# Two heads' matmuls into one PSUM bank: by token block, or head by head

## What is computed

```python
cb = jnp.einsum('bclgn,bcsgn->bcgls', c_c, b_c)
y_diag = jnp.einsum('bcgjls,bcsgjp->bclgjp', cb[:, :, :, None] * decay, xdt)
...
y = y + xs.astype(f32) * jnp.repeat(d_skip.astype(f32), SSD_HEAD_DIM)
g = (y * jax.nn.silu(z.astype(f32))).reshape(bsz, L, SSD_GROUPS, SSD_D_INNER // SSD_GROUPS)
g = g * lax.rsqrt(jnp.mean(g * g, axis=-1, keepdims=True) + EPS)
```

## Time and profile before

| | |
|---|---|
| median of 3 runs | 1215.65 us (1210.93 to 1218.96) |
| the profiled execution | 1215.65 us |
| its span, first to last instruction | 1214.0 us |
| mean granted clock of TensorE | 0.978 |
| TensorE busy over the span | 1153.8 us, 95% |
| VectorE busy over the span | 792.1 us, 65% |
| the change's function runs | from 64.7 to 233.4 us, eight times |

### The profile page before, as it was taken

One profiled execution on the slowest core, in us unless ns is written; L12 is line 12 of the kernel. 1 busy time (PEld: TensorE's weight loads), 2 busy tenths in 40 slices (PEclk: granted clock), 3 DMA queues, 4 the chain that ended last, 5 costly groups with the idle time before them and its releaser, 6 DMA issues.

```text
span 1214.0 us, 23710 instructions
## 1 busy us (share of the span) xinstructions
PE 1153.8 (95%) x8898; PEld 1091.7 (90%) x8898; DVE 792.1 (65%) x1219; ACT 646.9 (53%) x975; POOL 182.9 (15%) x134
## 2 busy tenths in 40 slices
PE   6999998999999999679898999999999999999998
PEld 5988898899999999556668999999998999999998
DVE  4999999868665453546546666555677578666543
ACT  5676677555554344457725555444544565555332
POOL 0343443317000001022302000000000211000000
PEclk9999999999999999889979999999999999999999
DMA  5644444384554544222204555555544455555553
GB/s 202 196 143 156 142 137 160 109 255 158 183 174 163 188 160 152 96 95 88 70 18 139 190 177 186 191 181 183 173 140 136 143 177 188 181 184 189 190 178 99
DMA packets 53224, 190.31 MB, mean 157 GB/s; under 512 B 5920, under 2 KB 7072, under 8 KB 53168
## 3 DMA queue, kind: packets, MB, share of 16 engines
q1 hardware_dynamic: 51408, 182.95, 45.4%
q0 software_dynamic: 1760, 6.59, 1.8%
HBM read 188.44 MB, written 1.08 MB: 156 GB/s over the span
## 4 chain that ended last, share of the span: by engine, by line
PE 77%; DVE 13%; ACT 5%; issue 3%; DVEq 1%; DMA 0%; ACTq 0%; POOL 0%; SPq 0%
PE lin L412 23%; PE lin L414 23%; PE lin L413 23%; DVE dd L1289 2%; DVE cv L1264 2%; DVE w_lo L1185 2%; PE lin L641 1%; PE ps L682 1%; PE ps L683 1%; ACT w_hi L824 1%; PE lin L639 1%; DVE mm L1314 1%; PE ps L756 1%; PE ps L779 1%; DVE x_tok L1306 1%
## 5 line engine op out<-in xcount | busy, mean ns | idle before, releaser
L1185 DVE TENSOR_TENSOR w_lo<-w_raw,w_hi 128x1024 fp32r<-128x1024 f32 x303 | 372.2, 1230 | 261.2 <-ACT w_hi L824 260.5
L824 ACT ACTIVATE w_hi<-w_raw 128x1024 fp32r<-128x1024 f32 (+2 forms) x343 | 355.0, 1040 | 265.3 <-PE lin L414 263.1
L412 PE MATMUL lin<-x_hi,w_hi 128*128 128x256 f32 (+1 forms) x1528 | 445.9, 292 | 10.9 <-DVE x_lo L1211 3.7
L414 PE MATMUL lin<-x_hi,w_lo 128*128 128x256 f32 (+1 forms) x1528 | 439.4, 288 | 0.0
L413 PE MATMUL lin<-x_lo,w_hi 128*128 128x256 f32 (+1 forms) x1528 | 438.8, 287 | 0.0
L412 PEld LDWEIGHTS lin<-x_hi,w_hi 128*128 128x128 f32 x1528 | 292.4, 191 | 15.5 <-DVE x_lo L1211 4.1
L413 PEld LDWEIGHTS lin<-x_lo,w_hi 128*128 128x128 f32 x1528 | 292.0, 191 | 1.5 <-issue 1.0
L414 PEld LDWEIGHTS lin<-x_hi,w_lo 128*128 128x128 f32 x1528 | 292.8, 192 | 0.0
L414 PE MATMUL lin<-hid_hi,w_lo 128*128 128x256 f32 (+1 forms) x768 | 218.2, 284 | 0.0
L413 PE MATMUL lin<-hid_lo,w_hi 128*128 128x256 f32 (+1 forms) x768 | 218.0, 284 | 0.0
L412 PE MATMUL lin<-hid_hi,w_hi 128*128 128x256 f32 (+1 forms) x768 | 217.5, 283 | 0.0
(11 more groups left out here) (252 smaller groups left out, 1522.1 us busy)
## 6 DMA issues: line engine op xcount, KB each, us to landing
w_raw<-w SPq DMA_DIRECT2D x343, 512.0 KB, 3.3
acs_bc<-acs_dram POOLq DMA_DIRECT2D x8, 544.0 KB, 4.9
bias_mask<-rpb POOLq DMA_DIRECT2D x4, 512.0 KB, 9.5
h<-h SPq DMA_DIRECT2D x4, 272.0 KB, 4.4
out<-h SPq DMA_DIRECT2D x8, 128.0 KB, 3.2
cst<-const SPq DMA_DIRECT2D x1, 784.0 KB, 8.8
vecs<-vec SPq DMA_DIRECT2D x1, 131.5 KB, 2.2
acs_dram<-y POOLq DMA_DIRECT2D x1, 34.0 KB, 2.3
```

What stands on the lines that cost most here:

```text
L412: mm3(o, wh, xh, start=first and i == 0, stop=False)
L414: ins = mm3(o, wl, xh, start=False, stop=last and i == kts - 1)
L824: a(w_hi[pg.slot][:, 0:n], w_raw[pg.slot][:, 0:n], ACT.Copy).then_inc(w_hi_done, pages)
L1185: tt(w_lo[pg.slot][:, 0:n], w_raw[pg.slot][:, 0:n], w_hi[pg.slot][:, 0:n].bitcast(F32), ALU.subtract)\
```

## The change

In each bank, the before kernel issues the first token block of both heads, then the second of both, then the third of both. The changed kernel issues the three blocks of one head, then the three of the other. The wait for `mm_done` is inside the head loop, with the same value for both heads. `y_done` is raised by the last matmul of the second head, as before.

```diff
-                    pe.wait_ge(mm_done, g.times(2, q + 1).value)
-                    halves = [(slice(e * HD, (e + 1) * HD), 2 * q + e) for e in range(2)]
-                    for rows, j in halves:
-                        nc.tensor.matmul(o[rows, 0:T], x_tok[:, 0, j * HD:(j + 1) * HD], mm[:, j, 0:T],
-                                         start=True, stop=False)
-                    for rows, j in halves:
-                        nc.tensor.matmul(o[rows, 128:T], x_tok[:, 1, j * HD:(j + 1) * HD], mm[:, j, T:416],
-                                         start=False, stop=False)
-                    for rows, j in halves:
-                        ins = nc.tensor.matmul(o[rows, 256:T], x_tok[0:META, 2, j * HD:(j + 1) * HD],
-                                               mm[0:META, j, 416:432], start=False, stop=True)
+                    for e in range(2):
+                        j = 2 * q + e
+                        pe.wait_ge(mm_done, g.times(2, q + 1).value)
+                        rows = slice(e * HD, (e + 1) * HD)
+                        cs = slice(j * HD, (j + 1) * HD)
+                        nc.tensor.matmul(o[rows, 0:T], x_tok[:, 0, cs], mm[:, j, 0:T], start=True, stop=False)
+                        nc.tensor.matmul(o[rows, 128:T], x_tok[:, 1, cs], mm[:, j, T:416], start=False, stop=False)
+                        ins = nc.tensor.matmul(o[rows, 256:T], x_tok[0:META, 2, cs], mm[0:META, j, 416:432],
+                                               start=False, stop=True)
                     ins.then_inc(y_done, 1)
```

## The result

| | before | changed |
|---|---|---|
| median of 15 runs each | 1216.53 us (1210.93 to 1218.96) | 1222.0 us (1216.36 to 1227.52) |
| ratio, 95% interval | | 1.0054 [1.0038, 1.0070] |
| the profiled execution, and its span | 1215.65 and 1214.0 us | 1221.69 and 1220.0 us |
| mean granted clock | 0.978 | 0.979 |
| one group's products, first to last | 2.15 us | 4.24 us |

Half a per cent slower, clear of the noise and within 1%, and within 0.6 us of the forecast of 1221.4. The two medians are 5.5 us apart, where 5.7 were forecast. The page of the changed kernel, beside the earlier trace rows: TensorE is busy 13.4 us longer over a span that is 6.0 longer.

What follows compares the result with a forecast made beforehand. VectorE was taken to pace the scan at 24.98 us a slot, until the lengthened loop through TensorE takes 25.88. Delays of 6.8 less 1.1 us of waits give 1215.65 + 5.7 = 1221.4 us; range 1215 to 1230.5.

Steps and rivals of the forecast that it cites:

- The pair costs what one costs: In `y_products`, two heads' matmuls run side by side; a lone head takes 1.075 us, a group 4.30 instead of 2.15.
- The 16-row matmul keeps the heads apart: In `y_products`, TensorE drains between 128 and 16 rows, so head 1 waits for head 0: +2.15 us per group.
- rival (a): In `y_products`, the heads still overlap despite the new order: no change, 1215.7 us; chance 0.13.
- The loop, 25.88 us: Scan slot: the chain TensorE, ScalarE, VectorE and back grows from 23.73 to 25.88 us, 0.90 longer than VectorE's pace.
- TensorE's own need, 25.07 us: Scan slot: TensorE's busy 22.92 us plus 2.15 makes 25.07, so it still waits 0.8 us at L492.
- rival (b): Scan: the loop is looser, nearly all added time is hidden and TensorE's 25.07 us counts: 1217.9 us; chance 0.12.
- Idle before L492 0.8 us, and no fall of the clock: Scan slots 2 to 7: TensorE idles about 0.8 us before L492 and the clock doesn't fall to 0.50.
- Slot by slot: Scan: delay grows to 0.6, 4.0, 4.7, then 6.8 us; vanished weight-load waits take off 1.1, leaving 5.7.
- The end: Behind the last group's L492 (244.44 us before) TensorE leads and everything shifts along: 5.7 us, 1221.4 us in all.
- (c): Scan: the clock falls to 1.2 GHz in every slot, 1.53 us each, 9.2 more: 1230.6 us; chance 0.10.
- (d): Scan: all added TensorE time is paid, 17.2 us over eight groups: 1232.9 us; chance 0.05.
- The second loop: Scan slot: the loop through VectorE's wait for bank 1's y (L1333) takes 25.5 us and decides nothing.

Runs made afterwards that it cites:

- The repeats: Kernel before with the first block of both heads issued once more, or twice more, per bank: ratios 1.0033 and 1.0026.
- three kernels of the table: Before, first block issued two times more; changed, 16-row matmuls last and first block issued twice; changed itself: slots 25.57, 25.67, 25.84 us.
- The changed kernel with GpSimd moved: Changed kernel with ScalarE's third page conversion behind the tap, one `w_lo` behind the clamp, another in the next slot: ratio to before 0.9958.
- the first repeat: Kernel before with the first block of both heads issued once more per bank: 3.06 us per group, ratio 1.0033.
- the second experiment: Changed kernel with the 16-row matmul made one of 128 rows, zeros added: ratio to before 1.0009.

## Why the prediction was right, step by step

- **The pair costs what one costs.** Right. One head alone takes 1.06 us (1.075 predicted) where two heads took 1.08. The group went to 4.24 us (4.30). The repeats show it from the other side: two more fp32 matmuls of 128x272 in a bank cost one's time, 0.91 us per group of two banks.
- **The 16-row matmul keeps the heads apart.** Right, and shown by taking it away from between them (2.16 us). Left out was a second reason: with 128 rows everywhere the new order still takes 2.47 us against 1.75, since head 1 starts only with head 0's third pass. That would have made rival (a) dearer than "no change" in the products, though not in the time.
- **The loop, 25.88 us.** Right to 0.04. By L492 of slots 3 to 7, 212.46 - 109.08 = 103.38 us in four slots (103.52 predicted, 100.16 before). That it is this loop is shown by cutting it with the clamp kept clear (25.84 to 25.21), and its constant by three kernels of the table (21.59 to 21.60 against 21.58). That VectorE sets the pace of the kernel before was right for its slots of 24.98 us alone; the two behind a fall of the clock were the loop's already, which is why they grow by 0.6 us and the others by 0.86.
- **TensorE's own need, 25.07 us.** A little high. The changed kernel with GpSimd moved shows 24.76 at products of 4.24, 0.3 less than forecast. The 22.92 of the earlier trace rows, which I added to, is of a slot that begins behind a wait, and in the kernel without waits this isn't paid; that this is the reason is likely and not shown. It decided nothing, but rival (b) rested on it, and by 24.76 it would have been cheaper still: no cost at all in the slots.
- **Idle before L492 0.8 us, and no fall of the clock.** Right: 0.78 to 0.82 in slots 3 to 7 (0.96 in slot 2), and 1.00 over 84 to 210 us.
- **Slot by slot.** Behind L492 of slot 2, the next slot took 0.58 us more (0.66 predicted), the four steady ones 3.22 together (3.36), slot 7 to 8 0.59 (0.7), and slot 8 to the last L492 0.89 (1.05, the products less the two waits; no wait on `g_lo` or `w_lo` is left there). Sum 5.28 us against 5.7. Each term was a little large, in part because the head's 1.075 was. The last L492 came at 249.03, not near 250.1, by these 0.4 us and by a lead of 0.69 (next point).
- **The end.** The 5.28 us aren't all of the 6.0 by which the spans differ. The changed kernel reached L492 of slot 2 0.69 us sooner, with a lead that it had before the first products, and took 1.44 us longer behind the last L492 (970.99 to 969.55), where its profile has 44.4 us at 1.2 GHz after 480 us and that of before 37.5. Both lie outside what was changed, and the second varies from run to run. So the 6.0 us between the two profiles are partly chance. The 5.5 between the medians of 15 runs are nearer to the 5.28 and bear the forecast better; that they meet the 5.7 to 0.2 us is within the noise of the medians.
- **Rivals.** (a) fell by the length of the products, (b) by the slots, (c) by the clock of 1.00. (d), all of it paid, fell by the first repeat, 0.91 us per group for nothing in the slots. (b) wasn't far off: two moves, of one conversion and of one `w_lo`, bring the slot from 25.84 to 25.21.
- **The second loop.** The one through VectorE's wait for `y` of bank 1 I had put at 25.5 us and as deciding nothing. It decided nothing, but the sum was wrong: the 13.9 from L1278 to L492 held the wait of 0.52 at the convolution. It measures 24.85. There is a wait of 0.67 us for this `y` in each of four slots, and the wait at the convolution behind it is there all the same. This loop became the one that paces as soon as the conversion was moved, which the forecast for that experiment didn't see.

## What to carry to other kernels

Two matmuls on the two column halves ran for the price of one here only where they stood close to each other in TensorE's program with no change of row count between them; issue them side by side, block by block. Ask what a slot's other loops hold before you price added time: 0.91 us per group cost nothing in the slots here, 2.09 (4.24 less 2.15) cost 0.86 per slot, and both follow from one sum along the chain from TensorE through the converting engine and back. When you sum such a loop, leave out the waits inside it. An engine's busy time is no lower bound of its pace when a neighbour's work holds its instructions up, as GpSimd's did VectorE's; and moving that work may mostly choose which instruction pays.

## What the runs showed of the hardware that I had not expected

- **Matmuls on different column halves start out of program order.** In the second experiment's rows head 1's L507 starts at 165.46, and head 0's L509, which stands before it in the program, at 165.70. The Trainium skill, TensorE: Matmul & The Clock Gate, section Part 3: Packing small matmuls — row/col tiling, says that matmuls are strictly in program order in start and end. The row differs in the starts, and it decides for these fp32 passes; the ends are modelled and tell nothing.
- **The view forward is limited.** With four passes of the other half ahead a head starts within 13 ns; with six it starts 0.51 us later, with the third of them (2.47 and 4.08 us a group in the two kernels). Whether it is passes that count, or instructions or something else, these three kernels don't tell.
- **Padding 16 rows to 128 was cheaper here than changing the row count.** It saves 0.40 us per group, which has two stretches of 16 rows, one in each bank (2.15 to 1.75), although the padded matmul multiplies eight times the rows: 0.10 us ahead of each stretch, 0.14 behind the first and 0.05 behind the second, where the `lin` chunk follows.
- **A 2.4 us `w_lo` on GpSimd can triple a VectorE clamp**, 0.45 to 1.42 us, and GpSimd's `w_lo` and `y` together double the mean `dd` of a slot (280 to 559 ns).
